# A layer step on one core: weight halves interleaved word by word, dense matmuls streamed in descending order, and the second activation buffer with staggered starts

## The reference

```
h = rmsnorm(x);  z = h @ w_in                       # 2048 -> some 16,500 columns, all mixers and gates
o_a = sparse attention (top-k keys by an indexer);  o_b = block-sparse attention;  o_c = retention, 8 heads
m = sig(g_a)*(o_a @ w_pa) + sig(g_b)*(o_b @ w_pb) + sig(g_c)*(o_c @ w_pc)
x = x + m @ w_out
y = gelu(causal_conv3(h2 @ ffn_up)) * (h2 @ ffn_gate)   # h2 = rmsnorm(x), 5504 columns
x = x + y @ ffn_down;   result = rmsnorm(x)
```

## Time and profile before

| | |
|---|---|
| median of 3 runs | 2369.67 us (2369.48 to 2369.94) |
| span of the profiled execution | 2368.6 us |
| TensorE matmul busy | 2354.7 us, 99% |
| weight loads busy | 2273.6 us, 96% |
| DVE busy | 1407.6 us, 59% |
| ACT busy | 919.6 us, 39% |
| GpSimd busy | 312.1 us, 13% |
| mean granted TensorE clock | 0.997 of full speed |

### The profile page before, as it was taken

How to read it: one execution, slowest core, us unless ns; L and a number is a source line. 1 busy time by engine, 2 the same in 40 slices (tenths; PEclk the granted TensorE clock), 3 DMA queues, 4 the chain that set the end, 5 groups by cost and what they waited for, 6 DMA issues and landing times.

```text
span 2368.6 us, 44628 instructions
## 1 busy us (share of the span) xinstructions
PE 2354.7 (99%) x17242; PEld 2273.6 (96%) x17242; DVE 1407.6 (59%) x2107; ACT 919.6 (39%) x1283; POOL 312.1 (13%) x629
## 2 busy tenths in 40 slices
PE   9999999999999999999999999999999999999998
PEld 9978999999999999999999999999999999999998
DVE  6535568899897545445456645666654456666433
ACT  5334343433433444334333344333333333333432
POOL 1135110000002222333200011000000000000000
PEclk9999999999999999999999999999999999999998
DMA  8448645556658988999776544444445544444553
GB/s 245 147 133 246 176 145 181 176 173 206 207 174 263 310 293 290 300 338 312 239 262 201 184 152 151 152 153 151 152 150 152 154 152 157 154 150 152 155 149 114
DMA packets 176307, 458.70 MB, mean 194 GB/s; under 512 B 25226, under 2 KB 75002, under 8 KB 175968
## 3 DMA queue, kind: packets, MB, share of 16 engines
q1 hardware_dynamic: 142192, 370.84, 48.8%
q0 software_dynamic: 26128, 75.67, 10.0%
q10 hardware_dynamic: 7776, 9.35, 1.1%
HBM read 425.27 MB, written 27.52 MB: 191 GB/s over the span
## 4 chain that ended last, share of the span: by engine, by line
PE 96%; DVE 1%; ACT 1%; issue 1%; DMA 1%; SPq 0%; DVEq 0%; ACTq 0%
PE ps L803 88%; PE ps L1077 1%; PE ps L1030 1%; PE ps L876 1%; PE ps L1060 1%; DMA w_raw<-in_w_in 1%; PE ps L1000 0%; ACT w_hi L1129 0%; PE ps L943 0%; PE ps L992 0%; PE ps L888 0%; PE ps L983 0%; PE ps L979 0%; DVE w_lo L1406 0%; PE ps L840 0%
## 5 line engine op out<-in xcount | busy, mean ns | idle before, releaser
L1406 DVE TENSOR_TENSOR w_lo<-w_raw,w_hi 128x1024 fp32r<-128x1024 f32 (+2 forms) x630 | 750.7, 1194 | 776.4 <-ACT w_hi L1129 773.1
L803 PE MATMUL ps<-h_hi,w_hi 128*128 128x320 f32 x3696 | 1160.4, 314 | 2.2 <-DVE h_lo L1569 1.7
L803 PE MATMUL ps<-h_lo,w_hi 128*128 128x320 f32 x3696 | 1131.6, 306 | 0.0
L803 PE MATMUL ps<-h_hi,w_lo 128*128 128x320 f32 x3696 | 1125.1, 304 | 0.0
L1129 ACT ACTIVATE w_hi<-w_raw 128x1024 fp32r<-128x1024 f32 (+2 forms) x630 | 649.3, 1033 | 804.8 <-PE ps L803 776.1
L803 PEld LDWEIGHTS ps<-h_hi,w_hi 128*128 128x128 f32 x3696 | 694.0, 188 | 33.0 <-issue 28.1
L803 PEld LDWEIGHTS ps<-h_lo,w_hi 128*128 128x128 f32 x3696 | 694.2, 188 | 0.5
L803 PEld LDWEIGHTS ps<-h_hi,w_lo 128*128 128x128 f32 x3696 | 693.8, 188 | 0.0
L803 PE MATMUL ps<-y_hi,w_hi 128*128 128x320 f32 x688 | 213.3, 310 | 0.0
L803 PE MATMUL ps<-y_lo,w_hi 128*128 128x320 f32 x688 | 210.5, 306 | 0.0
L803 PE MATMUL ps<-y_hi,w_lo 128*128 128x320 f32 x688 | 209.2, 304 | 0.0
(11 more groups left out here) (329 smaller groups left out, 2069.9 us busy)
## 6 DMA issues: line engine op xcount, KB each, us to landing
w_raw<-in_w_in SPq DMA_DIRECT2D x250, 512.0 KB, 5.0
w_raw<-in_ffn_up SPq DMA_DIRECT2D x86, 512.0 KB, 3.9
w_raw<-in_ffn_gate SPq DMA_DIRECT2D x86, 512.0 KB, 3.8
w_raw<-in_ffn_down SPq DMA_DIRECT2D x80, 448.0 KB, 3.4
kpg<-in_cache_b_k SPq DMA_DIRECT2D x128, 128.0 KB, 4.6
vpg<-in_cache_b_v POOLq DMA_DIRECT2D x128, 128.0 KB, 5.1
kpg<-in_cache_a_k SPq DMA_DIRECT2D x128, 128.0 KB, 4.8
vpg<-in_cache_a_v POOLq DMA_DIRECT2D x128, 128.0 KB, 5.0
```

The costliest lines, as they stand in the source:

```text
L803: mm = mmul(bank[q][:, 0:T], wp[:, s, cols], xp[:, x.k0 + k, :], start=(x.first and k == 0 and t == 0), stop=(x.last and k == x.nk - 1 and ...
L1406: tt(w_lo[:, s, 0:n], w_raw[:, s, 0:n], w_hi[:, s, 0:n].bitcast(F32), ALU.subtract).then_inc(w_lo_done, 1)
```

## The change

`w_hi` and `w_lo` become the even and the odd words of one buffer `w_two`: word 2c of a slot is the rounded weight of column c, word 2c+1 its remainder. ACT writes and DVE reads and writes every second word; a weight load reads every second word, 128 of them over 1024 bytes instead of 512. The start of `w_two` is where `w_hi` was (64 modulo 128), and all behind it stays where it was.

A dense pass takes its moving operand from column 319 down to column 0 and writes its PSUM bank from column 319 down to 0, so each result lands where it did. Weight columns are still named in ascending order.

The blocks of `y_hi` and `y_lo` no longer lie at multiples of 1280 bytes: block i starts 16 x (i // 3) bytes further on, so the starts modulo 128 are 0, 16, 32, ... 112, three blocks at each (the last has one). All other moving operands keep their places.

No instruction is added, removed or moved on any engine: the rows of TensorE, DVE, ACT, GpSimd and SP stand in the same order before and after, with the new buffer's name in them.

```diff
         w_raw = fix("w_raw", [P, SLOTS, KU * P])
-        w_hi = fix("w_hi", [P, SLOTS, KU * P], F32R)
+        w_two = fix("w_two", [P, SLOTS, KU * P, 2], F32R)
+        w_hi, w_lo = w_two[:, :, :, 0], w_two[:, :, :, 1]
         epsc = fix("epsc", [P, 1])
-        w_lo = fix("w_lo", [P, SLOTS, KU * P], F32R)
...
-        y_hi = at(0, 28160)("y_hi", [P, KF1, T], F32R)
-        y_lo = at(28160, 56320)("y_lo", [P, KF1, T], F32R)
+        y_hi = at(0, 28288)("y_hi", [P, KF1 * T + 28], F32R)
+        y_lo = at(28288, 56576)("y_lo", [P, KF1 * T + 28], F32R)
...
+        def feature(n):
+            i = n % KF1 * T + n % KF1 // 3 * 4
+            return y_hi[:, i:i + T], y_lo[:, i:i + T]
+
+        def moving(job, k):
+            if job.src == "y":
+                return feature(job.wk + k)
+            xh, xl = X[job.src]
+            return xh[:, k, :], xl[:, k, :]
...
-                    xh, xl = X[job.src]
                     for k in range(x.nk):
+                        xh, xl = moving(job, x.k0 + k)
                         cols = slice(k * P, (k + 1) * P)
...
                         for t, (wp, xp) in enumerate(((w_hi, xh), (w_hi, xl), (w_lo, xh))):
-                            mm = mmul(bank[q][:, 0:T], wp[:, s, cols], xp[:, x.k0 + k, :],
+                            mm = mmul(bank[q][:, 0:T][:, ::-1], wp[:, s, cols], xp[:, ::-1],
                                       start=(x.first and k == 0 and t == 0), stop=(x.last and k == x.nk - 1 and t == 2))
...
-                    fn(y_hi[:, job.n % KF1, :], yt[:, job.n % 2, :], ACT.Copy).then_inc(rounded, 1)
+                    fn(feature(job.n)[0], yt[:, job.n % 2, :], ACT.Copy).then_inc(rounded, 1)
...
-                    i = n % KF1
-                    tt(y_lo[:, i, :], yt[:, n % 2, :], y_hi[:, i, :].bitcast(F32), ALU.subtract).then_inc(split, 1)
+                    y_h, y_l = feature(n)
+                    tt(y_l, yt[:, n % 2, :], y_h.bitcast(F32), ALU.subtract).then_inc(split, 1)
```

More of the change, by code:

```diff
@@ L403, in build @@
         X = {"h": (h_hi, h_lo), "oc": (h_hi, h_lo), "h2": (h_hi, h_lo), "oa": (oa_hi, oa_lo), "ob": (ob_hi, ob_lo),
-             "m": (m_hi, m_lo), "y": (y_hi, y_lo)}
+             "m": (m_hi, m_lo)}
+        def feature(n):
[6 more added lines that the diff above has]
+            return xh[:, k, :], xl[:, k, :]
         z = (za, zb)
```

## The result

The changed kernel is slower: 2401.38 us (2401.08 to 2401.61) against 2369.81 us of the kernel before in the same session, a ratio of 1.0134 with a 95% interval of 1.0119 to 1.0148. I had forecast 2330 us; the time lies inside my range from 2246 to 2500, on the other side of no change.

A forecast was written before the change was run, and what follows sets the result against it. TensorE's own pace was taken as the bound, with 124 us of excess in dense passes; the 2368.6 us span less 39 us gave 2329.4, plus 1.1 us to the runs' median, 2330 us; range 2246 to 2500 us.

The forecast's parts named there:

- What bounds the kernel: Whole span: TensorE's own pace is the time, its matmuls covering 99%; dense passes at 144.45 ns with nothing between them.
- The floor: Dense passes: 320 columns at one clock each plus some 3 ns fixed would take 136 ns.
- The reading of the excess: Dense passes: the 8.4 ns above 136 ns are stalls of the moving stream against the weight stream, set by both addresses.
- the streams' term: All 14,688 dense passes: between 124 us less (whole excess gone) and 124 us more (twice the meetings); taken, 39 us less.
- The step that set the sign: Each block's three passes: durations of 310, 306 and 304 ns fall to the shortest, 8 ns a block, 39 us less.
- The reason for a gain: Dense passes: the old weight stream drifts against the moving stream and must meet it; streams stepping at like rates can stay apart.
- The single distance: 86% of the passes: h's alignment with outputs' and m's is one distance, 64 modulo 128, perhaps poor; hence a third of 124 us.
- more meetings at every pass: Rival, all 14,688 passes: weights upward and pass downward cross, excess doubles to 152.9 ns a pass, +124 us, 2494 us; chance 0.17.
- No change, by independent ports: Rival, dense passes: the excess is not the two streams', the pace stays 144.45 ns, 2369 us within 5 us; chance 0.13.
- half rate: Rival, dense passes: descending PSUM write or weight load over every second word halves the pace, adding 1 to 1.8 ms; chance 0.04.
- DVE as the bound: Rival, heads, then up and gate: every-second-word access adds 1.7 us a unit, 93 and 65 us lost, about 2527 us; chance 0.09.
- The y blocks: 2064 passes, 14%: new starts taken as nothing, at best 17 us within the 124; passes would differ by their eight distances.

## Why the prediction was wrong

- **What bounds the kernel** was right: TensorE's pace, no waits, DVE's and ACT's room untouched. The floor was right as well: a pass without excess takes 136 ns by my sum from the fp32 rows and 135.0 to 135.7 in the passes that stream one column or a window of up to 8 words. (By exactly two clocks a column those rows leave 2 ns above the columns rather than 3, which makes 135.3.)
- **The reading of the excess failed**: "I read the excess as stalls of the moving stream against the weight stream". A quarter of the load leaves it, 512 columns make it larger in proportion, and a moving window of 32 bytes takes it away. The bulk of it belongs to the moving stream alone, one clock in twelve columns once the addresses go beyond 32 bytes or a little more. The load's addresses share out only the small rest: a pass between 142 and 152 ns, a block between 433 and 448. So the 124 us were never open to a change of the weights' layout, and neither end of the streams' term had its ground.
- **The step that set the sign failed**: "All three passes come down to the duration of the shortest ... 39 us less". The passes drew level, as I said they would, but at 146.7 ns, above their old mean, not at the shortest. The term of -39 us measured +31.6. I had taken the three unequal durations of the earlier trace rows as two bad passes beside a good one. From start to start the three took 148.3, 143.3 and 141.7 ns, and they belong together: they come with loading `w_hi`, `w_hi`, `w_lo` in turn at these places, which as a whole is 6.7 ns a block better than the usual 440.0.
- **The reason for a gain failed**: that streams of like steps can stay apart. Woven weights with an ascending operand make the slowest kernel of all with the full computation, 448.0 ns a block on h2, and woven with descending is 440.0 at nearly any start: the pace that many other layouts have too.
- **The single distance "may be a poor one"** was the wrong way round. It is the best of all that were tried. It was not one distance either: `w_lo` starts at 96 modulo 128, not at 64, so the third pass has its own. And where I wrote "whatever the padding" the profile could have warned me: nearly all stages had the same 433.3 ns a block, so it told nothing of other starts.
- **The rivals**: more meetings at every pass had the right side and place, but its mechanism falls with the reading of the excess, and its size was four times too large (+124 us). No change, by independent ports, is wrong by 2.2 ns a pass. No pass came near half rate. DVE as the bound never came near: 1226 ns a unit. A descending PSUM write is free, as I took it, now shown by two kernels that differ in nothing else.
- **The Trainium skill's rules**: that the weight load takes no read bandwidth from the running matmul ("TensorE: Matmul & The Clock Gate", "Step-by-step: what each phase is for") agrees with the runs in the main, since a short load gives no time back, and disagrees in the small: the load's addresses alone move a pass from 144.4 to 146.7 ns (another start) or 148.8 (every second word). On single words two apart, DVE's 1226 ns a unit agree with "SBUF — State Buffer", "Door 1: The DMA port swizzle (why `[64,N]` ≈ `[32,N]`)", by which two hits in a 16-byte line are enough. They contradict "Vector Engine (DVE) Microarchitecture Reference", "5.2 Measured stream behaviour on trn2", by which full rate takes runs of two adjacent words.
- **The y blocks**: I took nothing; they cost 4.9 us when staggered alone, and in the changed layout give back 1.2 ns a block, 0.8 us. They do differ among themselves, as I had given for a sign: staggered alone, 438 to 444 ns over the eight starts. But the blocks at start 0 take 437.5 too, where without the stagger they take 433.3, so a block's own start does not fix its pace.

What stays open: why the addresses of load and operand move a pass by -2.2 to +2.7 ns about 146.7. No run gives the rule. They show that the addresses and the turn of the weight halves belong to it, that 128 bytes are not its period, and that something else belongs to it too, since one layout ran at 440.0 in one stage and 443.3 ns in another.

## What to carry to other kernels

When an engine is full and a pass takes longer than its columns, find out by width and by a repeated operand which of its streams the excess belongs to, before a layout is rebuilt round one of them. Where every stage of a kernel shows the same odd pace, its addresses may sit at a favourable point that a change of either operand's layout leaves; here every other start of weights or y cost 0.5 to 3.4% a block. One kernel can read a dozen such places at once, by stage, but a layout should be read in more than one stage: here the same one differed by 3.3 ns a block between two.

## What the runs showed of the hardware that was not expected

- A dense fp32r pass of 320 to 512 columns takes 1.083 clocks a column and 2.2 ns in the changed layout (146.7 ns for 320, 233.3 for 512), and one clock a column and some 2 ns where the moving addresses stay within 32 bytes (135.0 ns for 320).
- A weight load of 128 columns over every second word lasts 195 ns against 188, and loads that set the pace follow each other after 117 instead of some 110 ns. A PSUM write from the last column to the first costs nothing (2404.15 and 2403.72 us with the write either way).
- A pass of `w_hi` takes 148 ns while the next `w_hi` loads and 143 to 144 while `w_lo` loads, in the layout before, whichever half of the features it streams.
- The same addresses ran at 440.0 and at 443.3 ns a block in two stages of one kernel.
- ACT's copy slows by 8 to 11% when it writes every second word (1057 ns for 1024 words, 1171 in the changed kernel, 1144 in the woven, ascending one); DVE's subtraction, which reads one operand and writes at every second word, doesn't (1224 and 1226 ns).
- A start of 128 bytes further on changes the pace (444.4 for both halves, 436.7 for the remainders alone, against 433.3 ns).
